# Sums of squares in the projection stage: two rounded products in place of one fp32 product

## The reference

```python
def rmsnorm(x, g):
    y = xf * lax.rsqrt(jnp.mean(xf * xf, axis=-1, keepdims=True) + EPS)
    return (y * g.astype(jnp.float32)).astype(x.dtype)

h = rmsnorm(x, norm_attn[l])
z = h @ w_in[l]
qa, ka, va, cq, ckv, kr, qc, kc, vc = jnp.split(z, splits, axis=-1)
q = apply_axial_rope(rmsnorm(qa.reshape(B, S, N_HEADS_A, HEAD_DIM), q_gain), tabs)
k = apply_axial_rope(rmsnorm(ka.reshape(B, S, N_KV_A, HEAD_DIM), k_gain), tabs)
q = (rmsnorm(cq, q_gain) @ w_uq).reshape(B, S, N_HEADS_B, MLA_NOPE + MLA_ROPE)
kv = (rmsnorm(ckv, kv_gain) @ w_ukv).reshape(B, S, N_HEADS_B, MLA_NOPE + MLA_V)
```

## Time and profile before

| what | us |
|---|---|
| median of 3 runs (3009.47 to 3011.11) | 3010.93 |
| the profiled execution, its own time | 3007.72 |
| its span, first to last instruction | 3005.9 |
| PE busy in the span | 2899.8 (96%) |
| DVE busy | 2010.4 (67%) |
| ACT busy | 1313.2 (44%) |
| POOL busy | 474.9 (16%) |

### The profile page before, as it was taken

How to read it: one execution, slowest core, us unless ns; L and a number is a source line. 1 busy time by engine, 2 the same in 40 slices (tenths; PEclk the granted TensorE clock), 3 DMA queues, 4 the chain that set the end, 5 groups by cost and what they waited for, 6 DMA issues and landing times.

```text
span 3005.9 us, 36862 instructions
## 1 busy us (share of the span) xinstructions
PE 2899.8 (96%) x13560; PEld 2316.6 (77%) x13560; DVE 2010.4 (67%) x2316; ACT 1313.2 (44%) x1826; POOL 474.9 (16%) x250
## 2 busy tenths in 40 slices
PE   6999889999999999999999998899999999999998
PEld 4777656888778888888877785578887888888887
DVE  5877887992366655555678778889716555556555
ACT  3236788993322221222233287889823212222223
POOL 3111232223300000000131123322341000000002
PEclk8999999999999999999999999999999999999999
DMA  4455333323111211111135643234312111111101
GB/s 180 144 176 139 71 71 84 84 63 112 43 56 46 67 42 42 56 42 42 40 132 180 173 105 71 64 85 91 112 43 70 43 42 56 42 42 56 56 28 56
DMA packets 236372, 236.48 MB, mean 79 GB/s; under 512 B 59488, under 2 KB 199520, under 8 KB 236256
## 3 DMA queue, kind: packets, MB, share of 16 engines
q1 hardware_dynamic: 236256, 234.94, 27.4%
HBM read 184.04 MB, written 50.86 MB: 78 GB/s over the span
## 4 chain that ended last, share of the span: by engine, by line
PE 85%; DVE 8%; issue 4%; ACT 2%; DMA 1%; SPq 0%; POOL 0%; DVEq 0%; ACTq 0%
PE ps L1743 29%; PE ps L1758 16%; PE ps L1503 16%; PE ps L1593 8%; PE ps L1665 6%; PE ps L1631 3%; PE ps L1632 3%; DVE ps L1218 2%; PE ps L1627 2%; PE ps L1728 1%; PE ps L1529 1%; DVE xgl L1118 1%; PE ps L1678 1%; DVE prob L1287 1%; DVE rstd L1360 0%
## 5 line engine op out<-in xcount | busy, mean ns | idle before, releaser
L1593 PE MATMUL ps<-stack 128*128 128x512 f32 (+1 forms) x1152 | 347.3, 419 | 42.1 <-ACT prob L907 19.1
L1409 DVE TENSOR_TENSOR xT<-ps,xT 128x512 f32<-128x512 f32 x352 | 241.9, 691 | 214.4 <-PE ps L1758 214.2
L1665 PEld LDWEIGHTS ps<-cst,prob 128*128 128x128 f32 x2048 | 255.3, 142 | 90.2 <-issue 20.4
L1593 PEld LDWEIGHTS ps<-stack 128*128 128x128 f32 (+1 forms) x1152 | 206.9, 191 | 152.5 <-ACT prob L907 50.5
L1665 PE MATMUL ps<-cst,prob 128*128 128x128 f32 x2048 | 311.5, 275 | 7.8 <-issue 4.1
L907 ACT ACTIVATE prob<-ps,nmx 128x1024 f32<-128x1024 f32 x256 | 284.6, 1112 | 22.8 <-PE ps L1665 12.3
L1323 DVE TENSOR_TENSOR ptl<-ps,pth 128x512 fp32r<-128x512 f32 x384 | 259.1, 685 | 47.3 <-ACT pth L969 42.7
L1374 DVE SCALAR_TENSOR_TENSOR cv<-u,vec,cv 128x1024 f32<-128x1024 f32 x176 | 225.8, 1283 | 88.4 <-ACT cv L1046 78.2
L1058 ACT ACTIVATE ah<-cv 128x1024 fp32r<-128x1024 f32 x44 | 46.7, 1061 | 533.2 <-DVE cv L1387 533.2
L1743 PE MATMUL ps<-xgh,w0h 128*128 128x512 f32 x704 | 274.1, 389 | 2.6 <-ACT sq L1038 2.6
L1743 PE MATMUL ps<-xgl,w0h 128*128 128x512 f32 x704 | 273.9, 389 | 0.0
(11 more groups left out here) (225 smaller groups left out, 5587.8 us busy)
## 6 DMA issues: line engine op xcount, KB each, us to landing
wraw<-in_w_up SPq DMA_DIRECT2D x88, 512.0 KB, 4.7
draw<-in_w_down SPq DMA_DIRECT2D x22, 1024.0 KB, 4.9
stack<-ka_d SPq DMA_DIRECT2D x64, 256.0 KB, 5.4
wraw<-in_w_in SPq DMA_DIRECT2D x30, 512.0 KB, 4.0
vst<-v_d SPq DMA_DIRECT2D x48, 256.0 KB, 3.8
x_d<-xT SPq DMA_DIRECT2D x2, 4096.0 KB, 17.7
wraw<-in_w_out SPq DMA_DIRECT2D x16, 512.0 KB, 5.5
stack<-qc_d SPq DMA_DIRECT2D x64, 128.0 KB, 3.6
```

What stands on the lines that cost most here:

```text
L1409: ins = dve.tensor_tensor(xs, ps[:, 4 + j % 4, :], xs, ALU.add)
L1593: ins = pe.matmul(score_banks(i)[:, kh, :], st[q][0:rows, c0:c0 + P], st[k][0:rows, kh * HALF:(kh + 1) * HALF], start=n == 0, stop=n == le ...
L1665: ins = pe.transpose(ps[:, 4 + s % 2, m * P:(m + 1) * P], prob[:, b, m, s * P:(s + 1) * P], ident)
```

## The change

Each square is split like the other operands. ACT copies `sq`, rounded, into `sqh`; DVE subtracts it from `sq` into `sql` (which lies on the memory of `sq`); PE adds both with rounded matmuls against `ones_r` or `blk_r`, rounded copies of the two constant matrices that ACT makes once at the start. PE waits for `sq_lo`, DVE's count, where it waited for `sq_ready`, ACT's; before its first transpose it waits for `ones_rounded` too. The sum of squares for the layer's own norm (`sx`, L1542) stays in fp32.

```diff
         ident, ones, blk = cst[:, C_ID:C_ID + P], cst[:, C_ONE:C_ONE + P], cst[:, C_BLK:C_BLK + P]
         eps = cst[:, C_EPS:C_EPS + 1]
+        ones_r, blk_r = sb(ctx, "ones_r", [P, P], F32R), sb(ctx, "blk_r", [P, P], F32R)
...
         ph1 = ExitStack()
         ra, rb_ = sb(ph1, "ra", [P, 2, T]), sb(ph1, "rb_", [P, 2, T])
-        z, sq, r = sb(ph1, "z", [P, 2, T]), sb(ph1, "sq", [P, T]), sb(ph1, "r", [P, T])
+        z = sb(ph1, "z", [P, 2, T])
+        same = ExitStack()
+        sql = sb(same, "sql", [P, T], F32R)
+        same.close()
+        sq, r = sb(ph1, "sq", [P, T]), sb(ph1, "r", [P, T])
         e = sb(ph1, "e", [P, 2, T])
         rg = sb(ph1, "rg", [P, 4, T], F32R)
         wqh, wql = sb(ph1, "wqh", [P, 2, 384], F32R), sb(ph1, "wql", [P, 2, 384], F32R)
         wkh, wkl = sb(ph1, "wkh", [P, 512], F32R), sb(ph1, "wkl", [P, 512], F32R)
+        sqh = sb(ph1, "sqh", [P, T], F32R)
         ph1.close()
...
         w_hi, w_lo, proj_done, z_ready = sem("w_hi"), sem("w_lo"), sem("proj_done"), sem("z_ready")
         sq_ready, sq_free, job_ready, job_free = sem("sq_ready"), sem("sq_free"), sem("job_ready"), sem("job_free")
+        sq_hi, sq_lo, ones_rounded = sem("sq_hi"), sem("sq_lo"), sem("ones_rounded")
         r_free, latent_ready, out_ready = sem("r_free"), sem("latent_ready"), sem("out_ready")
         roped, split_hi, split_lo, ring_stored = sem("roped"), sem("split_hi"), sem("split_lo"), [sem(f"ring_stored{i}") for i in range(SLOTS)]
...
                 hi_item(0, n, wait=False)
             act.wait_ge(const_loaded, 32)
+            act.activation(ones_r[:, :], ones, ACT.Copy)
+            act.activation(blk_r[:, :], blk, ACT.Copy).then_inc(ones_rounded, 1)
             for t in range(KT):
                 gained(t, gain0, (x_final, t + 1))
...
                             act.wait_ge(sq_free, l * len(SQUARED) + n)
                         act.activation(sq[0:rows, :], (ckv if t == 2 else z[:, t % 2, :])[0:rows, :], ACT.Square).then_inc(sq_ready, 1)
+                        act.wait_ge(sq_ready, l * len(SQUARED) + n + 1)
+                        act.activation(sqh[0:rows, :], sq[0:rows, :], ACT.Copy).then_inc(sq_hi, 1)
                     if t - 1 in A_TILES:
                         hi_event("z", t - 1)
...
                     dve.wait_ge(z_ready, l * NT + t + 1)
+                def lo_squares(t):
+                    n, rows = SQUARED.index(t), CQ1 if t == 1 else P
+                    dve.wait_ge(sq_hi, l * len(SQUARED) + n + 1)
+                    dve.tensor_tensor(sql[0:rows, :], sq[0:rows, :], sqh[0:rows, :].bitcast(F32), ALU.subtract).then_inc(sq_lo, 1)
                 def rope(v, tab, r0, r1, shift, other):
...
                 dve.wait_ge(r_free, l + 1)
                 evacuate(0)
+                lo_squares(0)
                 evacuate(1)
                 dve.wait_ge(vec_loaded, l * 16 + 16)
...
                     step(dve.tensor_tensor(vec[:, a:a + CQK], vec[:, a:a + CQK], vec[:, b:b + CQK], ALU.mult))
                     step(dve.tensor_reduce(small[:, i:i + 1], vec[:, a:a + CQK], AX.X, ALU.add))
+                lo_squares(1)
                 step(dve.tensor_tensor(small[:, 5:6], vec[:, V_SUB:V_SUB + 1], vec[:, V_LI + 1:V_LI + 2], ALU.mult))
                 evacuate(2)
                 wait_root("scq")
                 step(dve.reciprocal(r[:, :], r[:, :]))
+                lo_squares(2)
                 step(latent(0, 0, vec[:, V_CQG:V_CQG + 1], P))
                 latent(1, 1, vec[0:CQ1, V_CQG + 1:V_CQG + 2], CQ1).then_inc(latent_ready, 1)
...
                 dve.wait_ge(roped, l + 1)
                 lo_event("kr", 1)
+                lo_squares(4)
                 for t in range(5, NT):
                     evacuate(t)
+                    if t in A_TILES:
+                        lo_squares(t)
                     for kind, a in EVENTS.get(t, []):
                         if kind == "z" and a in A_TILES:
...
         def _(pe):
             pe.wait_ge(const_loaded, 32)
+            pe.wait_ge(ones_rounded, 1)
             for t in range(KT):
                 if t == 0:
...
                     return ps[:, 4 + 2 * (j % 2) + b, :]
-                def squares_sum(j, n, lhsT, src, start, stop):
-                    pe.wait_ge(sq_ready, l * len(SQUARED) + n + 1)
-                    for b in range(2):
-                        ins = pe.matmul(bank(j, b), lhsT, src[:, b * HALF:(b + 1) * HALF], start=start, stop=stop)
+                def squares_sum(j, n, lhsT, rows, start, stop):
+                    pe.wait_ge(sq_lo, l * len(SQUARED) + n + 1)
+                    for i, part in enumerate((sqh, sql)):
+                        for b in range(2):
+                            ins = pe.matmul(bank(j, b), lhsT[0:rows, :], part[0:rows, b * HALF:(b + 1) * HALF], start=start and i == 0, stop=stop and i == 1)
                     return ins
...
                             ins = pe.matmul(bank(j, b), ones, rstd[:, b * HALF:(b + 1) * HALF], start=True, stop=True)
                     elif kind == "scq":
-                        squares_sum(j, 1, ones[0:64, :], sq[0:64, :], False, True).then_inc(sq_free, 1)
+                        squares_sum(j, 1, ones_r, CQ1, False, True).then_inc(sq_free, 1)
                         ins = None
                     elif kind in ("sckv", "sa"):
                         n = 2 if kind == "sckv" else SQUARED.index(a)
-                        squares_sum(j, n, ones if kind == "sckv" else blk, sq[:, :], True, True).then_inc(sq_free, 1)
+                        squares_sum(j, n, ones_r if kind == "sckv" else blk_r, P, True, True).then_inc(sq_free, 1)
                         ins = None
                     elif kind == "uq":
...
                         pe.wait_ge(fence, l * 5 + 5)
                     if t == 1:
-                        squares_sum(job_no("scq", 0), 0, ones, sq[:, :], True, False).then_inc(sq_free, 1)
+                        squares_sum(job_no("scq", 0), 0, ones_r, P, True, False).then_inc(sq_free, 1)
                     for kind, a in JOBS.get(t, []):
                         job(kind, a)
```

## The result

| kernel | median, us | lowest to highest, runs | ratio to before, 95% interval |
|---|---|---|---|
| before | 3010.20 | 3007.46 to 3011.11, 4 | |
| changed | 3044.30 | 3040.52 to 3048.56, 4 | 1.0119, 1.0105 to 1.0133 |

The change costs 34.1 us where 42 were forecast: slower, and by less than the sum said. The profiled execution of the changed kernel took 3040.52 us with a span of 3038.7; that of before has 3005.9, so the two traces differ by 32.8 us. The profiled execution of the change is the fastest of its four, 3.8 us under their median, so the traces show a little less than the medians.

A forecast was written before the change was run, and what follows sets the result against it. PE and DVE were taken to bound the projection stage's end together, so delays to DVE's in-order chain delay everything behind. Start 3.9 plus 2 x 19.0 a layer gave 41.9 us, hence 3053 us; range 3029 to 3067.

The forecast's parts named there:

- The start: Before PE's first transpose: waiting for both rounded constants delays PE by 3.9 us, and the loop behind passes it on.
- Tile 0: First sum of a layer: PE waits 2.4 us for the subtraction; back at 0 by 96, +0.1 taken for DVE.
- Tile 4: DVE's subtraction stands behind ten steps: PE idles 6.7 us, half clock loses 2.2, the reciprocal begins at +4.2.
- Tile 6: PE arrives after the subtraction and doesn't wait; DVE, waiting for projection 7, takes over PE's shift: +7.9.
- Tile 8: The first value subtraction queues behind the new one; its store frees ACT's ring slot late: ACT's tile 9 copy at +13.5.
- Tiles 10 and 11: Square, copy and subtraction chains delay PE's sum to +15.9, at half pace, and the reciprocal of tile 10 to +19.0.
- The end of the stage: DVE runs without a wait to tile 13's evacuation; PE waits some 2.7 us before attention; layer +19.0.
- worse: Rival: half clock also after tile 0 and at attention's start, subtractions caught behind POOL (+8): 3058 to 3070; chance 0.16.
- GpSimd and the subtractions: Subtractions could lie behind POOL's at the SBUF port; none does in the walk, nothing added; +8 if two a layer did.
- Only the work counts: Rival: waits are hidden, only six subtractions a layer on DVE's busy chain and the start cost: 3030; chance 0.11.
- The clock stays full: Rival: PE keeps full clock through its stalls, layer 16.1 us: 3047; inside the forecast's own range, chance 0.68 either way.
- The products win: Rival: DVE is never behind, so only PE's 12.8 us saving and the start's 3.9 count: 3002; chance 0.03.

The follow-up runs named there:

- e3: Changed kernel with e1's edit, without DVE's subtraction: PE waits for ACT's copy, second matmul pair uses a zero matrix, low part left out; 3006.97 us, ratio 0.9994.
- e8: Changed kernel with e1's edit, all waits kept, DVE's subtraction over only 8 of 1024 columns, low part left out of the sum; 3026.65 us, ratio 1.0064.
- e11: Changed kernel with e1's edit, all arithmetic kept: tile 4's square, copy and subtraction moved earlier, subtractions of tiles 8 and 11 later; 3023.46 us, ratio 1.0043.
- e5: Changed kernel with tile 4's sum undone: whole squares in fp32 on PE, no copy or subtraction there; 3032.19 us, ratio 1.0081.
- e2: Changed kernel with e1's edit, rounded product alone: square written straight to sqh, no copy or subtraction, second matmul pair against zeros; 3002.01 us, ratio 0.9976.
- e12: Changed kernel with 24 unread matmuls put on PE right ahead of its wait for tile 4's subtraction, the wait kept; 3039.43 us, ratio 1.0098.
- e7: Changed kernel with DVE's order turned at tile 8: low parts of the value splits ahead of the subtraction; 3041.60 us, ratio 1.0113.
- e6: Changed kernel with the sums of tiles 10 and 11 undone: whole squares in fp32, no copy or subtraction there; 3031.51 us, ratio 1.0074.
- e9: Changed kernel with e1's edit, DVE's full subtraction kept, but PE waits only for ACT's copy; low part left out of the sum; 3027.29 us, ratio 1.0066.
- e10: Changed kernel with e1's edit, one rounded product: square written straight to sqh, two matmuls per sum, no copy or subtraction; 2997.92 us, ratio 0.9962.
- e1: Changed kernel with PE's wait for the rounded matrices moved from before its first transposes to ahead of the first sum of squares; 3041.99 us, ratio 1.0110.
- e4: Changed kernel with e1's edit, the subtraction issued by GpSimd among its weight splits instead of by DVE; 3028.12 us, ratio 1.0067.

## Why the prediction was right, and where it was off

**The verdict and the mechanism held.** DVE's place in its order, not PE's work, sets the end: e3, e8 and e11 show it. The size is 9 us too high, and one of the forecast's own signs says so: the end of the first stage was to be at +16 to +22 without the start, and is at +15.2. Four terms are off, and not all the same way, so that the sum is nearer than they are. The product saves what was said: in the change a rounded sum of two pairs stands between the pair at 93.97 and the next projection at 95.33, 0.90 us from 94.43, against 1.71 from rows 3. The copy takes 1.06 and the subtraction 1.226, as costed from rows 5.

**The start failed.** The forecast put PE's first transpose at 19.25; it is at 18.94. But "the loop behind it ... passes the delay on" was wrong, and "nothing in it is waiting for something else" is the step: DVE's first low parts of the input had themselves been slow beside GpSimd, and the first two took 3.0 us less once they began later. The first projection matmul moved by 0.04 us. Rows 4 show only where the transposes begin; whether a loop passes a delay on is read from where it ends.

**Tile 0** was right in size: PE waits 2.51 us where 2.4 were forecast. The reciprocal of the key latents is 1.1 us late against the first one (17.84 us behind it, 16.75 before), since the subtraction of tile 2 stands between the two. The forecast let DVE get that back ahead of tile 4, and it does: in e5, where all but tile 4's sum is as in the change, z4 stands at -0.8, as in e2.

**Tile 4** was right: 6.33 us of wait against 6.7, the clock at 0.62 for 5 us, worth 2.1 by e12 where 2.2 were taken. From the root sum of x, 0.94 us earlier in the change (54.90 against 55.84), to the reciprocal of z4 the loss is 141.88 - 138.56 + 0.94 = 4.3, as forecast (4.2). e5 gives 10 us for it in the two layers.

**Tile 6**: forecast +7.9, and in the trace DVE's evacuation of tile 7 moved from 156.84 to 163.74, +6.9, or 7.8 with the 0.94.

**Tile 8 was mis-sized.** The low part of the first value split, begun at 178.38 before (rows 9), begins at 190.95, +12.6, near the 13.5 forecast; PE's sum of tile 8 begins behind 4.06 us of idle time (3.9 forecast), and PE is granted 0.72 behind it. But ACT's copy of tile 9 is at 195.53 against 186.50, +9.0:

```profile
195.53 1.06 ACT L856 ACTIVATE rg<-z 128x1024 fp32r<-128x1024 f32 x1 [4.88 <-DMA v_d<-rg]
```

The step that failed is "its store frees the ring slot", with the store taken to need as long as before. From the start of that low part to ACT's copy were 8.1 us before (186.50 - 178.38) and are 4.6 in the change (195.53 - 190.95). Before, the sync engine issued the four value stores close behind one another, in 5.53 us; in the change they are spread over 7.92 us, in which it waits 5.1 us for DVE's low part. First before, then the change, then the change's wait:

```profile
179.67 5.53 SPq L506 DMA_DIRECT2D v_d<-rg  x4
```

```profile
186.65 7.92 SPq L513 DMA_DIRECT2D v_d<-rg  x4
```

```profile
SPq L513 <- DVE rg L1207: 5.1, 1, 5.1
```

e7 takes the subtraction out of the way of these low parts, and there the interval is 8.2 us again (195.75 - 187.51), with the stores issued in 6.08 us:

```profile
188.81 6.08 SPq L513 DMA_DIRECT2D v_d<-rg  x4
...
195.75 1.06 ACT L856 ACTIVATE rg<-z 128x1024 fp32r<-128x1024 f32 x1 [2.93 <-DMA v_d<-rg]
```

So it is the holding back that shortens it. Of the 3.5 us, 1.2 are DVE's: held back, the two low parts run one behind the other in 2.35 us, while before the second waited for its high part and ended 3.6 us behind the start of the first. The other 2.3 are the store's: from the end of the second low part to ACT's copy are 4.5 us before, 4.6 in e7 and 2.2 in the change. That the last store then has less in front of it, since the first had gone already, fits these rows; no run takes that apart from the rest. In layer two the copy is at +9.7 against the first latents' reciprocal. In the sum the term is 3.5 to 4.5 us a layer too dear.

**Tiles 10 and 11** were right in size: from z9's split to the reciprocal of z10 the loss grows from 9.0 to 13.8, by 4.8, where 5.5 were forecast; e6 takes away 4.9 there. But PE's wait at tile 10, forecast as 5 to 7 us, is 1.65, and the sum behind it doesn't go at half pace, as the forecast had it:

```profile
218.44 0.70 PE L1554 MATMUL ps<-sqh,blk_r 128*128 128x512 f32 x2 [1.65 <-DVE sql L1173]
```

DVE came some 4.5 us sooner than forecast, by the term of tile 8. In layer two the wait is 3.24 us, the pair behind it takes 1.19, and z10 is at +15.4: by then layer two has lost the 1.5 us that it loses more than layer one.

**The end of the stage** had a term that the forecast kept for its rival "worse". PE waited 4.05 us before attention's first matmul, not 2.7, and was then granted 0.63 from 256 to 261 us. So 13.9 at the evacuation of tile 13 (256.77 against 242.90) became 15.2 at the first maximum.

```profile
258.16 2.90 PE L1618 MATMUL ps<-stack 96*128 96x512 f32 x6 [4.05 <-issue]
```

**The sum again.** Forecast 3.9 + 19.0 + 19.0 = 41.9. Measured by the traces: 0 + 15.2 + 16.7 for the stages, 4.1 from layer one's first maximum to layer two's first latent reciprocal (1311.8 us against 1307.7), and -3.1 for the rest of layer two, where nothing was edited: 32.8 but for rounding. The forecast had both of the last two at 0, and said within 3 us; over the profiles of all kernels here that rest of layer two lies between 1286.4 and 1291.5 us (1290.1 before, 1287.0 in the change), so its -3.1 says nothing of the change.

**GpSimd and the subtractions.** The forecast weighed the Trainium skill's SBUF — State Buffer, section Who interferes with whom, against the change, and added nothing because GpSimd would not be at work then. The trace agrees with that walk: the longest of 16 subtractions took 1.227 us. It was at the start of the program that GpSimd counted: DVE's step beside it took 3.28 us, and 1.28 without it.

**The rivals.** "Only the work counts" (3030) is refused by e8: without the work 18.7 us remain. "The clock stays full" is refused by the rows at 134 us and by e12. "The products win" needed DVE out of the way; e2 shows that it is then true, with 3002 us. That this is to the microsecond the figure given for it is luck: the sum is another one (7.8 of 12.8 us saved, and no start term).

**What stays open.** The stretch from layer one's first maximum to layer two's latents holds no edit but the sums of tiles 0 and 1 of layer two. It takes 1306.0 to 1308.6 us in before, e2, e3, e8, e9 and e10 and 1310.3 to 1316.7 in the change and in e1, e4, e5, e6, e7, e11 and e12, one profile each. The second group are the kernels that send the low parts through PE, but that does not separate them: up to the reciprocal of layer two's root (1282.6 us before, 1285.9 in the change) e3 and e10 without low parts take 1284.0 and 1284.1, e4 and e6 with them 1284.0 and 1284.4. What goes with it is PE's clock. In e7 (4.6 us longer than before up to that root) the 10 us that begin 440 us behind the first maximum were granted 0.66; in the change (3.3 us longer) 0.83, and before 1.00. Behind the root, e7's sum of tile 0 ran at half pace too (a pair in 1.22 us, 0.73 in the change). What lowers the clock in attention in one kernel and not in another, no run here shows.

This is also where the gains of e7 went: its stages are 8.0 us shorter than the change's, but its first latents' reciprocal is 2.7 us later, the stretch between the stages 2.7 longer and the rest 1.0, so its span is 1.6 us shorter.

## What to carry to other kernels

Work that is split over engines costs its handovers where an engine works in order: before adding an instruction that waits for a neighbour, find what is queued behind it, and put it behind as much of that as the consumer allows. e11 won back over half of the loss without changing one operation. A cheaper product is worth only what the engine that feeds it leaves over, and a delay at the start of a loop counts only if the delayed engine also ends the loop last.
